# Two loads of the last stage moved ahead of the wait for the last experts' stores

## The reference, cut to what matters

```python
x = x + concat([o_att, o_conv]) @ w_out                 # x2 in the kernel
h = rmsnorm(x, norm_ffn)
x = x + hier_moe(h, ...)                                # x3: two experts for each token, 16 experts
e = rmsnorm(p @ w_ple_proj, ple_norm)                   # ple_norm: the "gain" of the last stage
x = x + sigmoid(x @ w_ple_gate) * e
```

## Time and profile before

| | us |
|---|---|
| median of 3 runs (lowest, highest) | 618.79 (618.16, 618.94) |
| the profiled execution's own time | 619.54 |
| its span, first to last instruction | 617.7 |

### The profile page before, as it was taken

How to read it: one execution, slowest core, us unless ns; L and a number is a source line. 1 busy time by engine, 2 the same in 40 slices (tenths; PEclk the granted TensorE clock), 3 DMA queues, 4 the chain that set the end, 5 groups by cost and what they waited for, 6 DMA issues and landing times.

```text
span 617.7 us, 8603 instructions
## 1 busy us (share of the span) xinstructions
PE 606.9 (98%) x3120; PEld 494.9 (80%) x3120; DVE 410.9 (67%) x765; ACT 337.4 (55%) x607; POOL 59.2 (10%) x78
## 2 busy tenths in 40 slices
PE   9999999999999999999999999999999999999997
PEld 5878888888887787878878887678888888778886
DVE  5522356253543466566677798899999999588873
ACT  6762222231313475564555475789999998861211
POOL 0010000000000000101001112331211211210000
PEclk9999999999999999999999999999999999999999
DMA  8933305231221513123133775999999999675611
GB/s 327 380 108 146 102 2 178 95 99 34 69 69 34 172 42 137 45 93 101 42 132 104 255 223 198 396 378 396 410 411 412 410 412 388 252 301 214 221 53 69
DMA packets 37019, 122.13 MB, mean 198 GB/s; under 512 B 5673, under 2 KB 6569, under 8 KB 36945
## 3 DMA queue, kind: packets, MB, share of 16 engines
q1 hardware_dynamic: 31120, 108.38, 47.7%
q0 software_dynamic: 4896, 12.59, 5.3%
q10 hardware_dynamic: 960, 0.61, 0.4%
HBM read 108.94 MB, written 18.91 MB: 207 GB/s over the span
## 4 chain that ended last, share of the span: by engine, by line
PE 91%; DVE 3%; DMA 2%; ACT 2%; issue 1%; SPq 0%; POOLq 0%; DVEq 0%; POOL 0%
PE bank L490 25%; PE bank L492 24%; PE bank L491 24%; PE bank L1872 7%; PE bank L1899 3%; PE bank L1918 3%; PE bank L1880 2%; PE bank L2039 1%; PE bank L2197 1%; DMA moe_rows<-moe_y,slot_row 1%; DMA pick<-moe_rows 1%; ACT s L935 1%; PE bank L1949 1%; DMA moe_x<-h_rows,slot_token 1%; DVE s L1356 0%
## 5 line engine op out<-in xcount | busy, mean ns | idle before, releaser
L490 PE MATMUL bank<-w_split,h_T_prompt 128*128 128x512 f32 x191 | 76.2, 399 | 0.0
L492 PE MATMUL bank<-w_split,h_T_prompt 128*128 128x512 f32 x191 | 74.5, 390 | 0.0
L491 PE MATMUL bank<-w_split,h_T_prompt 128*128 128x512 f32 x191 | 74.4, 390 | 0.0
L485 DVE TENSOR_TENSOR w_split<-w_raw,w_split 128x1024 fp32r<-128x1024 f32 x33 | 40.3, 1221 | 40.9 <-ACT w_split L480 40.8
L490 PE MATMUL bank<-w_split,moe_xT 128*128 128x512 f32 x120 | 48.4, 404 | 0.0
L492 PE MATMUL bank<-w_split,moe_xT 128*128 128x512 f32 x120 | 47.0, 391 | 0.0
L491 PE MATMUL bank<-w_split,moe_xT 128*128 128x512 f32 x120 | 46.8, 390 | 0.0
L490 PEld LDWEIGHTS bank<-w_split,h_T_prompt 128*128 128x128 f32 x191 | 36.0, 189 | 8.4 <-issue 1.6
L935 ACT ACTIVATE s<-s,mn 128x512 f32<-128x512 f32 (+1 forms) x48 | 30.9, 645 | 21.5 <-DVE mn L1356 21.5
L492 PEld LDWEIGHTS bank<-w_split,h_T_prompt 128*128 128x128 f32 x191 | 35.8, 188 | 7.7
L491 PEld LDWEIGHTS bank<-w_split,h_T_prompt 128*128 128x128 f32 x191 | 35.9, 188 | 7.0
(11 more groups left out here) (304 smaller groups left out, 1411.4 us busy)
## 6 DMA issues: line engine op xcount, KB each, us to landing
w_raw<-in_w_moe SPq DMA_DIRECT2D x32, 512.0 KB, 14.2
w_raw_room<-in_w_moe SPq DMA_DIRECT2D x30, 512.0 KB, 16.4
w_raw_more<-in_w_moe SPq DMA_DIRECT2D x30, 512.0 KB, 16.8
w_raw<-in_w_in SPq DMA_DIRECT2D x23, 512.0 KB, 5.5
pick<-moe_rows SPq DMA_DIRECT2D x12, 512.0 KB, 4.9
w_raw<-in_w_out SPq DMA_DIRECT2D x8, 512.0 KB, 3.5
toep<-bias_table SPq DMA_DIRECT2D x4, 896.0 KB, 8.7
x_row<-in_x SPq DMA_DIRECT2D x6, 512.0 KB, 9.4
```

The lines of the kernel that those rows point to most:

```text
L485: nc.vector.tensor_tensor(W[:, u % WS, 1], raw(u)[0], f(W[:, u % WS, 0]), ALU.subtract).then_inc(lo_done, 1)
L490: nc.tensor.matmul(out, hi, whi, start=first, stop=False)
L491: nc.tensor.matmul(out, lo, whi, start=False, stop=False)
L492: return nc.tensor.matmul(out, hi, wlo, start=False, stop=last)
```

## The change

Two loads and their waits move up, ahead of the wait for the last scatters, and a new wait, for the low part of the first half of the first tile's x3T, stands before them. Everything else is as it was.

```diff
             x2_again(1)
+            sp.wait_ge(d_x3t, 1)
+            x2_again(2)
+            sp.wait_ge(d_hot, TILES)
+            sp.dma_start(gain[:], gains[2]).then_inc(gain_ld, 16)
             sp.wait_ge(y_st[0], 16 * 7)
             sp.wait_ge(y_st[1], 16 * 8)
             pick(1)
-            x2_again(2)
             sp.wait_ge(pe_x3, 2)
             pick(2)
-            sp.wait_ge(d_hot, TILES)
-            sp.dma_start(gain[:], gains[2]).then_inc(gain_ld, 16)
             x2_again(3)
             sp.wait_ge(d_x3, 4)
             pick(3)
```

## The result

| | before | with the change |
|---|---|---|
| median of 18 runs each, us | 618.71 | 620.91 |
| lowest, highest | 618.16, 619.66 | 619.32, 622.89 |
| ratio | | 1.0038 [1.0027, 1.0048] |
| second comparison (21 and 12 runs) | 618.56 | 620.04 |
| ratio | | 1.0020 [1.0011, 1.0029] |

What follows compares the result with a forecast made beforehand. TensorE, busy 98%, was bound by a chain of last scatter, then pick(1), leaving it idle 0.92 us. Terms 0 + 0 + 1.4 + 0 = +1.4 us on the 618.8 median gave 620.2 us, range 619.5 to 620.8.

Steps and rivals of the forecast that it cites:

- 1.: On SyncE's queue, the new wait is over at 541.50 us, before the scatter lands: cost 0.
- 2.: Moved loads as seen from pick(1), the second tile's picks: flight unchanged at 5.1 us, so 0.
- rival B: Loads fill the DMA hole, queue stays warm, pick(1) lands up to 0.9 us earlier: 617.9 to 618.5 us; chance 0.11.
- 3.: Load rows share the last DMA engine with the last expert's scatter, which lands later: +1.4 us, bounds 0 and 2.6.
- 4.: Pick(2), gain and later loads after the move: nobody waited for them, all land ahead of use, gain 0.
- rival C: Both loads' rows delay the last scatter by 2.3 to 2.6 us: 621.3 us, TensorE's stall 3.4 us; chance 0.12.
- Rival A: Last scatter untouched by the loads, pick(1) lands at 550.9, time 618.8 us; chance 0.20 together with D.
- D: New wait on SyncE's queue comes too late for the DMA hole: 618.8 us; chance no more than 3 in 100.

Runs made afterwards that it cites:

- the filler: Changed kernel with six unread matmuls added on TensorE ahead of its wait for the second tile's first half: 620.91 us (1.0038).
- the later turns: Second tile's turns written later, behind three more matmuls (0.7 us): on the changed kernel 619.27 us (1.0008), on the kernel before 618.19 us (0.9992).
- the loads put between: Changed kernel with both loads behind the wait for the scatters and ahead of pick(1), without the new wait: 622.81 us (1.0070).
- the halves: Changed kernel with one load moved only: third tile's rows alone 618.56 us (1.0004), gain alone 619.18 us (1.0009).
- three loads: Changed kernel with the fourth tile's rows moved up too, 1.5 MB instead of 1.0: 622.49 us (1.0063).

## Why the prediction was right, and where it wasn't

Forecast 620.2, +1.4 us; measured +2.3 and +1.2. The medians are 620.91, 0.1 us above the forecast's own range of 619.5 to 620.8, and 620.04, inside it. The direction and the size are right, the mechanism isn't: the prediction says that it is wrong "if the scatter lands at its old time with loads beside it", and that is what the traces of the change show.

1. The new wait costs nothing: right. It is over at 541.3, SyncE has issued both loads by 542.1 and waits again until 545.06.
2. "I take its flight as unchanged": this step failed. It rested on rival B's remark that the loads are done at about 546 to 547, and on pick(1) being issued no sooner. I had let the scatter be late by 1.4 us to get there. With the scatter on time, gain is still in flight for 2.5 us behind pick(1)'s issue, and pick(1) flies 6.5 and 7.3 us instead of 5.1. With the filler it is 6.3, and with the later turns 5.3, so the loss varies from nearly nothing to 2.2 us. That queueing behind the loads is its cause is supported by the loads put between (7.6 us from the queue's release) and by the halves; what makes one execution with the same order lose and another not is open.
3. The scatter, +1.4 us: not in the two traces of the change (6.38 and 6.32 us; kernels without the loads in front 6.1 to 6.4), nor with the filler or the later turns (6.2 and 6.3), but +1.4 in the kernel without the new wait. The last engine's backlog of the earlier trace rows wasn't the rule that I made of it. That such a backlog falls differently in the next execution would explain it, but isn't shown.
 The sum of 2 and 3 came out near 1.4 us, and that is in part luck: 1.4 was worked out from rows of loads among the scatter's last rows on one engine, and what was measured is a wait of pick(1). Over the four traces with the change's order the sum grew by 1.4, 2.1, 0.9 and 0.1 us. Both terms do stand for the same thing, bytes that the hole can't swallow and that pass ahead of pick(1): 1 MB needs 2.5 us, and in the first trace a good half of that is left.
4. Pick(2), gain, the rest: right. TensorE has no wait behind the turn.

What was mis-sized is the clock. I gave its fall 2 in 100, inside rival C, and tied it to a stall of about 3 us. In the changed kernel it came in 8 of 30 runs, traced once at a stall of 2.6 us, and costs 1.6 us. The 7 such runs of the first comparison are 2.1 us above the others (medians 622.38 and 620.25), which is 0.8 us on the average of its 18 runs: most of the difference between 1.4 and 2.3 us. Also, the trace of before was a slow sample: its stall of 0.92 us isn't in the fastest runs (618.1 us; the traces of 616.4 to 616.5 without a stall are of executions of 618.15 to 618.3 us), so part of the added delay was free there, which I had allowed for with "some tenths".

Rival B: refuted, the time went up and not down, and pick(1) flew 5.3 to 7.3 us with the loads in the change's order. Rival A: right on the mechanism of the scatter, which was untouched, and wrong on the time, 618.8. C: its time was reached by 7 of 18 runs and passed, but not by its mechanism; in the trace of such a run the scatter takes 6.3 us, and the time is in pick(1)'s flight and the clock. D: refuted, the loads do fill the hole.

## What to carry to other kernels

An idle stretch of the DMA engines has a size in bytes. What counts for what is put in it is how much of it is still in the engines when the next awaited load is issued, not when it was issued itself: here 0.5 MB cost 0.2 to 0.6 us and 1 MB 1.2 to 2.3. A load that is needed on the path shouldn't have bulk transfers ahead of it in its queue that nobody is waiting for; before, both loads were behind it and cost nothing. And TensorE's own work, moved in front of a wait that varies, is worth its length in the executions that stall, and may be worth the clock as well: 0.7 us of it gave 0.7 to 1.8 us. Added work is paid in every run, moved work isn't. And a loss that was read from one trace should be looked for in a second one: here five traces with the same megabyte moved have it in two different places and at 0.1 to 2.1 us.

## What the runs showed of the hardware

Stalls of TensorE of 2.6, 2.8 and 3.2 us (the change, the loads between, three loads) were each followed, 0.6 to 1.2 us after TensorE had gone on, by a stretch at a granted clock of 0.50, which cost 1.6 us in all three: 66.8 us from the turn to the end against 65.1 to 65.2. The stalls of 0.9, 1.6 and 1.8 us in other traces were not. The length of the stall isn't shown to be all that decides: untraced executions of 621.87 and 622.18 us kept a clock of 1.000. Two half megabytes that cost 0.2 and 0.6 us alone cost 1.2 to 2.3 us together. And the delay by the loads fell on the scatter in one trace (7.8 us, pick(1) 4.9) and on the load behind it in two others (6.4 and 6.3 us, pick(1) 6.5 and 7.3), while with the same order of loads pick(1) took 5.3 us in a further one.
